# Sparse attention in a decoder step: page products divided among the single steps of the dense products

## The chip, the cores and the metric

The kernel runs on one core of a Trainium2 chip. The metric is the device time of one execution in microseconds. A core has five engines with instruction queues of their own: TensorE (PE in the profile; PEld is its weight load), VectorE (DVE), ScalarE (ACT), GpSimd (POOL) and SyncE (SP). Each queue is worked off in order; engines wait for each other through semaphores. TensorE's clock is granted at one of two levels, 2.4 GHz (1.00 in the profile) or 1.2 GHz (0.50).

## The reference

One inference step of a four-layer decoder for a prompt of 512 tokens and 8 sample sequences of one token, model width 1024. The layers' mixers are a gated recurrence, sparse attention, a state-space mixer and the recurrence again; each is followed by a squared-ReLU MLP. The change is in the sparse attention, layer 1:

```python
q, k, v, qi, ki, wi = split(x @ w_in)          # 8 heads of 128; indexer: 8 heads of 64
ki = layer_norm(ki)
score = sum_h wi[h] * relu(qi[h] . ki)         # indexer scores, per query and key
sel = top_k(score)                             # keys that this query may use
logits = q . K[sel] / sqrt(128) + rel_bias[bucket(distance)]
o = softmax(logits) . V[sel] @ w_out
```

For the prompt, K and V are those of the prompt itself. For a sample they are 256 cached positions, in two pages of 128 that a page table names, and its own. A sample's page products are matrix times vector: for each sample, head and page, a 128 x 128 block of the page times one query column (logits), and later a block of the value page times one column of probabilities (values).

## The kernel before

Activations stand with features on the partitions and the 520 tokens (512 and 8) in the free dimension. A dense product is cut into *tiles* of 128 output features. A tile takes one *chunk* of weights, 128 x 1024, and has eight *steps* `k` of 128 input features. To keep float32 accuracy in the faster float32r format, weights and activations are split into a high and a low part; a step is six TensorE instructions (two halves of 260 tokens, three products each, lines L1702 to L1704). `tile(n, T)` issues a whole tile, `part(n, T, ks)` only the steps `ks`.

Weight chunks come in order on SyncE's DMA queue into two `raw` slots (L416). For each chunk ScalarE makes the high part (`high_at`, L595), GpSimd the low part (`low_at`, L450); after that the raw slot is free and the load two chunks on may start. ScalarE also copies finished tiles out of PSUM (L865), so its queue, written out by hand, mixes splits of coming chunks, copies and the attention's own work, and each waits for the one ahead of it.

The sparse-attention layer is the function `dsa`. Counted by tiles:

- Tiles 0 to 4 are indexer keys and queries. After them TensorE makes the keys' mean and mean square (L1850, L1852) and waits for VectorE's variance (`ki_var`). It then issues the head weights of the indexer, 3 query blocks x 8 steps, with eight moving columns each (L1859), the same for the samples (L1863), and the products that spread the relative-position bias into rows (L1867, L1868). ScalarE waits for these, copies the head weights (L899, L901) and the bias rows (L904, L905) out and issues the DMA that writes the bias rows to DRAM (L907); only then does its loop over tiles 5 to 28 begin, with `high_at` of chunk 8. Tile 5 comes after all this on TensorE.
- Tiles 6 to 8 (attention queries) alternate, two steps at a time, with the prompt's index products (L1879), whose ReLUs ScalarE makes (L875) and VectorE weighs and sums; tiles 9 to 12 with the samples' (L1888, L1895).
- Tiles 13 to 20 are the attention keys. After each whole tile comes `page_logits(n)`, the 16 page products of sample `n` (L1906, two instructions each, 32 in the profile). VectorE works on the top-k meanwhile.
- Tiles 21 to 28 are the attention values, an iteration `it` each: two steps, then `slot(s)` with attention products of the prompt (logits L1929, turns L1941, values L1961). From `it` = 3 on, `page_values(it - 3)` (L1917, 32 instructions) stands ahead of the tile; the last three pages follow in the tail, after the last tile.

A sample's two pages fill one of two page slots. GpSimd issues their loads (`kv_pages`, L500) after it has split the chunk that is queued before them, and once `pages_used` tells that the sample two before has been used.

The lines that the change touches are in `dsa`:

Of the kernel before, what the change touches and what calls it, by code (L numbers as in the profile page):

```python
# [24 lines left out]
P = 128  # L25
D = 1024
KT = D // P
NP_ = 512
NS = 8
N = NP_ + NS  # L30
NH2 = N // 2
TB = NP_ // P
# [4 lines left out]
HEADS = 8  # L37
# [8 lines left out]
HN = HEADS * NS  # L46
# [59 lines left out]
def trunk(nc, I, O, kinds=KINDS):  # L106
# [3 lines left out]
    def sb(name, shape, dt=F32, c=ctx):  # L110
        return c.enter_context(nc.sbuf_tensor(name, shape, dt))

    def sem(name):
        return ctx.enter_context(nc.semaphore(name))
# [3 lines left out]
    c = ExitStack()  # L118
# [3 lines left out]
    c = ExitStack()  # L122
# [20 lines left out]
    c = ExitStack()  # L143
# [4 lines left out]
    c = ExitStack()  # L148
# [7 lines left out]
    c = ExitStack()  # L156
# [3 lines left out]
    c = ExitStack()  # L160
# [11 lines left out]
    c = ExitStack()  # L172
    mixB = sb("mixB", [P, KT, N], F32, c)
# [3 lines left out]
    pg = sb("pg", [P, 2, 2, D], F32, c)  # L177
# [4 lines left out]
    c = ExitStack()  # L182
# [91 lines left out]
    mb = ctx.enter_context(nc.psum_tensor("mb", [P, 4, 512], F32))  # L274
# [4 lines left out]
    tile_out = sem("tile_out")  # L279
# [31 lines left out]
    pg_loaded = [sem("b_pg_loaded0"), sem("b_pg_loaded1")]  # L311
# [75 lines left out]
    def low_count(n):  # L387

        before = sum(min(max(n - a, 0), b - a) for a, b in by_dve)
        if any(a <= n < b for a, b in by_dve):  # L390
            return w_low_dve, before + 1
        return w_low, n - before + 1
# [1293 lines left out]
    def _(pe):  # L1686
# [4 lines left out]
        def chunk(low, slot, T, hi, lo, k0, start, stop, split=None, ks=range(KT)):  # L1691

            if 0 in ks:
                pe.wait_ge(*low)
            for k in ks:
                if split is not None:
                    pe.wait_ge(xl_ready, split + k + 1)
                w = slice(k * P, (k + 1) * P)
                for half in range(2):
                    t = slice(half * NH2, (half + 1) * NH2)  # L1700
                    first, last = start and k == 0, stop and k == KT - 1
                    pe.matmul(bank(T, half), wh[:, slot, w], hi[:, k0 + k, t], start=first, stop=False)  # L1702
                    pe.matmul(bank(T, half), wh[:, slot, w], lo[:, k0 + k, t], start=False, stop=False)  # L1703
                    ins = pe.matmul(bank(T, half), wl[:, slot, w], hi[:, k0 + k, t], start=False, stop=last)  # L1704
            return ins

        def tile(n, T, split=None):

            if T >= 2:
                pe.wait_ge(tile_out, T - 1)  # L1710
            chunk(low_count(n), n % SPL, T, xh, xl, 0, True, True, split).then_inc(chunk_done, 1)

        def part(n, T, ks, split=None):

            if 0 in ks and T >= 2:
                pe.wait_ge(tile_out, T - 1)
            ins = chunk(low_count(n), n % SPL, T, xh, xl, 0, True, True, split, ks)
            if KT - 1 in ks:
                ins.then_inc(chunk_done, 1)
# [121 lines left out]
        def dsa(y, c0, t0):  # L1841
# [9 lines left out]
            for b in range(2):  # L1851
                ins = pe.matmul(mb[:, 2 + b, 0:NH2], ones_idx[:], rl[:, 0, b * NH2:(b + 1) * NH2], start=True, stop=True)  # L1852
            ins.then_inc(ki_stats, 1)

            pe.wait_ge(ki_var, 1)
            pe.wait_ge(x_ready, 16 * y["i"])
            for qb in range(1, TB):
                for k in range(KT):
                    pe.matmul(mb[:, 0, (qb - 1) * IH:qb * IH], x[:, k, qb * P:(qb + 1) * P], wwi[:, k, :],  # L1859
                              start=k == 0, stop=k == KT - 1)  # L1860
            for a in range(2):
                for k in range(KT):
                    ins = pe.matmul(mb[0:4, 1, a * NS:(a + 1) * NS], wwi[:, k, 4 * a:4 * a + 4], x[:, k, NP_:N],  # L1863
                                    start=k == 0, stop=k == KT - 1)
            ins.then_inc(wi_psum, 1)

            pe.matmul(mb[0:HEADS, 2, :], relb[:, 0:8], oh_p[:, 0:512], start=True, stop=True)  # L1867
            pe.matmul(mb[0:HEADS, 3, 0:ROW - 512], relb[:, 0:8], oh_p[:, 512:ROW], start=True, stop=True  # L1868
# [27 lines left out]
                                    stop=n == NS - 1 and a == 1)  # L1896
                ins.then_inc(s8_ready, 1)

            def page_logits(n):

                pe.wait_ge(pg_loaded[n % 2], 32 * (n // 2 + 1))
                pe.wait_ge(tile_out, t0 + 13)
                for g in range(2):
                    for h in range(HEADS):
                        col = g * HN + h * NS + n
                        ins = pe.matmul(mb[:, 3, col:col + 1], pg[:, n % 2, g, h * P:(h + 1) * P],  # L1906
                                        mixB[:, h, NP_ + n:NP_ + n + 1], start=True, stop=True)
                ins.then_inc(pages_used, 1)

            def page_values(n):  # L1910

                slot_ = (NS + n) % 2
                pe.wait_ge(pg_loaded[slot_], 32 * ((NS + n) // 2 + 1))
                for h in range(HEADS):
                    col = h * NS + n
                    for g in range(2):
                        ins = pe.matmul(pagev[:, col:col + 1], pg[:, slot_, g, h * P:(h + 1) * P],  # L1917
                                        sptt[:, g * HN + col:g * HN + col + 1], start=g == 0, stop=g == 1)
                ins.then_inc(pages_used, 1)

            def logits(u):
                h, qb = UNITS[u]
# [42 lines left out]
            def slot(s):  # L1965

                it, i = s // 4, s % 4
                if i == 1 and 1 <= it <= HEADS:
                    turn_values(it - 1, min(s - TURN, NU))
                if VALUE <= s:  # L1970
                    values(s - VALUE)
                if s < NU:
                    logits(s)
                if TURN <= s < NU + TURN:
                    turn(s - TURN)

            tile(c0 + 5, t0 + 5)
            pe.wait_ge(ki_ready, 1)
            pe.wait_ge(rows_out, 2)
            for c in range(6, 9):  # L1980
# [8 lines left out]
            for c in range(9, 13):  # L1989
                for i in range(4):  # L1990
                    n = 2 * (c - 9) + i // 2
                    part(c0 + c, t0 + c, (2 * i, 2 * i + 1))
                    (sample_dots, sample_sums)[i % 2](n)
            for c in range(13, 21):
                tile(c0 + c, t0 + c)
                page_logits(c - 13)
            for it in range(HEADS):
                c = 21 + it
                if it == 0:
                    pe.wait_ge(sneg_ready, 1)  # L2000
                    pe.wait_ge(s8_out, 1)
                    pe.matmul(mb[0:HN, 1, 0:SK], relb[:, 8:72], oh_p[:, ROW:ROW + SK], start=True, stop=False)
                    pe.matmul(mb[0:HN, 1, 0:SK], rep8, s8, start=False, stop=True).then_inc(sz_ready, 1)
                if it == 1:
                    pe.wait_ge(sz_out, 1)
                    pe.wait_ge(sprod, 1)
                    pe.matmul(mb[0:HN, 1, PAST:SK], sprodt, ones[:, 0:1], start=True, stop=True)
                    pe.wait_ge(slog, 1)
                    for g in range(2):
                        ins = pe.transpose(mb[0:HN, 1, g * P:(g + 1) * P], ltok[:, g * HN:(g + 1) * HN], ident[:])  # L2010
                    ins.then_inc(sy_ready, 1)
                if it == 2:
                    pe.wait_ge(sp_ready, 1)
                    for g in range(2):
                        pe.transpose(mb[:, 1, g * HN:(g + 1) * HN], sl[:, g * P:(g + 1) * P], ident[0:HN, 0:HN])
                    pe.matmul(mb[:, 1, P:P + HN], ones[0:HN, :], sdiag, start=True, stop=True).then_inc(spt_ready, 1)
                if it >= 3:
                    pe.wait_ge(spt_out, 1)
                    pe.wait_ge(sbc_out, 1)
                    page_values(it - 3)  # L2020
                for i in range(4):
                    part(c0 + c, t0 + c, (2 * i, 2 * i + 1))
                    slot(4 * it + i)
            for s in range(NU, NU + VALUE):
                slot(s)
                if s < NU + 3:
                    page_values(s - NU + 5)
# [3 lines left out]
        for y in plan:  # L2031
            ln = 2 * y["i"]
            c0, t0 = y["c"], y["t"]
# [21 lines left out]
            if y["kind"] == 1:  # L2055
                dsa(y, c0, t0)
                tail, ttail = c0 + 29, t0 + 29
# [77 lines left out]
            for half in range(2):  # L2135
# [17 lines left out]
                with pe.Fori(0, KT // 2) as i:  # L2153
                    for m in range(2):
                        T = t2 + m
                        pe.wait_ge(tile_out, i * 2 + T - 1)
                        for b in range(2):
                            n = c2 + 2 * m + b
                            low, count = low_count(n)
                            pe.wait_ge(h_ready, g1 + KT * (b + 1))  # L2160
                            ins = chunk((low, i * 4 + count), n % SPL, T, hh, hl, 8 * b, b == 0, b == 1)
# [131 lines left out]
```

## Time and profile before

| | |
|---|---|
| median of three runs | 3060.54 us (3057.29 to 3063.38) |
| profiled execution | 3046.29 us, span 3044.6 us |
| TensorE busy | 2844.6 us, 93% of the span |
| VectorE, ScalarE, GpSimd busy | 51%, 34%, 34% |
| mean granted clock of TensorE | 0.952 |
| DMA, mean | 97 GB/s |
| stage of tiles 13 to 20 | 940.79 to 1029.35 us of the span |
| iterations with a page, tiles 24 to 28 | 1065.63 to 1148.29 us of the span |

Times within the profile are microseconds from the start of the span. A busy TensorE is not one at full speed: the granted clock of a stretch has to be read beside it. Matmuls overlap, so the distance from one start to the next is what an instruction costs, not its length.

### The profile page before, as it was taken

To read this page: it belongs to the slowest core of one execution; us is meant where nothing else is said; L and a number is where in the kernel's file an instruction comes from. 1 tells how busy PE (TensorE), PEld (TensorE's weight loads), DVE (VectorE), ACT (ScalarE), POOL (GpSimd) and SP (SyncE) were. 2 spreads that over 40 slices of the span, in tenths; PEclk is the share of its full clock that TensorE was granted. 3 is DMA by queue.
4 is the path that set the end of the run, shared out by engine and by line. 5 is a ranking of instruction groups with operands and counts; after the bars stand their busy time and mean duration, and the time that the engine had idled before them with its cause. 6 is when DMAs were issued, how large, how long until landed. Compare 5 with 4: busy or idle time off the path is not lost. (4 is left out here: it accounts for less than half of the span.)

```text
span 3044.6 us, 54973 instructions
## 1 busy us (share of the span) xinstructions
PE 2844.6 (93%) x22296; PEld 2752.8 (90%) x22296; DVE 1550.8 (51%) x2208; ACT 1045.7 (34%) x1612; POOL 1037.7 (34%) x537
## 2 busy tenths in 40 slices
PE   7999799999889999999994798999999998899997
PEld 7999799999868999899994698999989997899997
DVE  4555356062235532789697936606245554471442
ACT  4555342122331343422214434212245455331222
POOL 2000164444523224544441145444530001554442
PEclk9999899999988898999996999999999998899999
DMA  4222123222253332224245522322232221232221
GB/s 147 82 82 72 37 84 97 90 90 96 91 103 117 141 124 72 93 95 145 90 158 187 170 74 76 97 92 94 91 95 79 78 85 51 64 97 91 92 94 63
DMA packets 125232, 294.81 MB, mean 97 GB/s; under 512 B 11058, under 2 KB 58674, under 8 KB 124946
## 3 DMA queue, kind: packets, MB, share of 16 engines
q1 hardware_dynamic: 56592, 206.10, 21.0%
q10 hardware_dynamic: 63362, 68.68, 7.5%
q0 software_dynamic: 5120, 17.83, 1.6%
q8 instruction: 110, 1.80, 0.2%
q14 instruction: 48, 0.39, 0.0%
HBM read 255.87 MB, written 36.70 MB: 96 GB/s over the span
## 5 line engine op out<-in xcount | busy, mean ns | idle before, releaser
L450 POOL TENSOR_TENSOR wl<-raw,wh 128x1024 fp32r<-128x1024 f32 x325 | 807.6, 2488 | 840.0 <-ACT wh L587 507.4
L1702 PE MATMUL lp<-xh,wh 128*128 128x260 f32 x3712 | 1077.8, 290 | 14.3 <-POOL wl L450 4.8
L1704 PE MATMUL lp<-xh,wl 128*128 128x260 f32 x3712 | 1061.0, 286 | 0.0
L1703 PE MATMUL lp<-xl,wh 128*128 128x260 f32 x3712 | 1058.4, 285 | 0.0
L1702 PEld LDWEIGHTS lp<-xh,wh 128*128 128x128 f32 x3712 | 712.6, 192 | 35.8 <-issue 22.4
L1703 PEld LDWEIGHTS lp<-xl,wh 128*128 128x128 f32 x3712 | 712.0, 192 | 0.4
L1704 PEld LDWEIGHTS lp<-xh,wl 128*128 128x128 f32 x3712 | 711.3, 192 | 0.0
L1702 PE MATMUL lp<-hh,wh 128*128 128x260 f32 x2048 | 578.6, 283 | 4.4 <-DVE r L1187 4.4
L1704 PE MATMUL lp<-hh,wl 128*128 128x260 f32 x2048 | 578.6, 283 | 0.0
L1703 PE MATMUL lp<-hl,wh 128*128 128x260 f32 x2048 | 576.8, 282 | 0.0
L1702 PEld LDWEIGHTS lp<-hh,wh 128*128 128x128 f32 x2048 | 385.4, 188 | 5.0 <-issue 5.0
L1704 PEld LDWEIGHTS lp<-hh,wl 128*128 128x128 f32 x2048 | 385.2, 188 | 0.0
L1703 PEld LDWEIGHTS lp<-hl,wh 128*128 128x128 f32 x2048 | 385.0, 188 | 0.0
L595 ACT ACTIVATE wh<-raw 128x1024 fp32r<-128x1024 f32 x213 | 223.9, 1054 | 261.8 <-PE lp L1704 123.5
L1674 DVE TENSOR_TENSOR hl<-lw,hh 128x520 f32 x128 | 292.4, 2284 | 15.8
L587 ACT ACTIVATE wh<-raw 128x1024 fp32r<-128x1024 f32 x176 | 185.8, 1056 | 268.7 <-PE lp L1704 208.9
L462 POOL TENSOR_TENSOR xl<-mixA,xh 128x520 fp32r<-128x520 f32 x16 | 20.8, 1332 | 671.0 <-ACT xh L601 671.0
L1130 ACT ACTIVATE lw<-lp 128x520 f32<-128x520 f32 x124 | 75.0, 605 | 447.9 <-PE lp L1704 425.1
L1189 DVE SCALAR_TENSOR_TENSOR r<-x,lp 128x520 f32<-128x520 f32 x56 | 39.0, 696 | 344.3 <-PE lp L1704 320.6
L1672 DVE TENSOR_TENSOR lw<-lw 128x520 f32<-128x520 f32 x128 | 115.4, 902 | 193.4 <-ACT lw L1130 189.3
L1729 PE MATMUL lp<-xh,wh 128*128 128x260 f32 x352 | 104.0, 320 | 75.4 <-ACT xh L601 31.7
L1729 PEld LDWEIGHTS lp<-xh,wh 128*128 128x128 f32 x352 | 77.2, 219 | 80.1 <-ACT xh L601 33.4
(352 smaller groups left out, 3546.5 us busy)
## 6 DMA issues: line engine op xcount, KB each, us to landing
raw<-in_wstream SPq DMA_DIRECT2D x389, 512.0 KB, 3.5
s<-in_s_in ACTq DMA_DIRECT2D x16, 512.0 KB, 5.7
out_hg_s<-s ACTq DMA_DIRECT2D x16, 512.0 KB, 3.3
pg<-in_kpages POOLq DMA_DIRECT2D x16, 512.0 KB, 5.3
pg<-in_vpages POOLq DMA_DIRECT2D x16, 512.0 KB, 5.4
s_q<-pqb ACTq DMA_DIRECT2D x8, 640.0 KB, 3.9
qn<-s_q ACTq DMA_DIRECT2D x8, 640.0 KB, 5.4
s_rot<-lw ACTq DMA_DIRECT2D x8, 512.0 KB, 2.6
```

What stands on the lines that cost most here:

```text
L450: pool.tensor_tensor(wl[:, s, :], raw[:, r_, :], wh[:, s, :].bitcast(F32), ALU.subtract).then_inc(w_low, 1)
L462: pool.tensor_tensor(xl[:, m, :], src[:, m, :], xh[:, m, :].bitcast(F32), ALU.subtract).then_inc(xl_ready, 1)
L587: act.activation(wh[:, s, :], raw[:, r_, :], ACT.Copy).then_inc(w_high, 1)
L595: act.activation(wh[:, n % SPL, :], raw[:, n % RAW, :], ACT.Copy).then_inc(w_high, 1)
L1130: act.activation(halves(lw[:, 6 + c % 2, :]), out_banks(T, half == 0 and i is first and c == 2), ACT.Relu).then_inc(tile_out, 1)
L1189: dve.scalar_tensor_tensor(halves(r[:, m, :]), halves(x[:, m, :]), ALPHA, src, ALU.mult, ALU.add).then_inc(tile_out, 1)
L1672: link.step(dve.tensor_tensor(hq, lw[:, 6 + c % 2, :], lw[:, 6 + c % 2, :], ALU.mult))
L1674: dve.tensor_tensor(lo, hq, hi.bitcast(F32), ALU.subtract).then_inc(h_ready, 1)
L1702: pe.matmul(bank(T, half), wh[:, slot, w], hi[:, k0 + k, t], start=first, stop=False)
L1703: pe.matmul(bank(T, half), wh[:, slot, w], lo[:, k0 + k, t], start=False, stop=False)
L1704: ins = pe.matmul(bank(T, half), wl[:, slot, w], hi[:, k0 + k, t], start=False, stop=last)
L1729: pe.matmul(out, wh[:, slot, w], xh[:, k, t], start=k == 0, stop=False)
```

## The change

Three edits on TensorE's queue; the instructions are the same ones in another order, and no other engine's program changes.

1. Page logits: after each single step of tiles 13 to 20 come the products of one head (two page products, four instructions), in place of all 16 products after the tile. The wait for the sample's pages stands ahead of head 0, so after the tile's first step.
2. Page values: in the iterations 3 to 7, one head's products after each step, in place of all of them ahead of the tile. The three pages of the tail stay as they were.
3. Index head weights: steps 0 and 1 of tile 5 are put ahead of the wait for `ki_var`; the other six steps stand singly between groups of head-weight products, four steps of a query block each, and around the two halves of the samples' products. The bias-row products come after all of tile 5.

```diff
+            part(c0 + 5, t0 + 5, (0, 1))
             pe.wait_ge(ki_var, 1)
             pe.wait_ge(x_ready, 16 * y["i"])
-            for qb in range(1, TB):
-                for k in range(KT):
+
+            def head_weights(qb, ks):
+
+                for k in ks:
                     pe.matmul(mb[:, 0, (qb - 1) * IH:qb * IH], x[:, k, qb * P:(qb + 1) * P], wwi[:, k, :],
                               start=k == 0, stop=k == KT - 1)
-            for a in range(2):
+
+            def sample_head_weights(a):
+
                 for k in range(KT):
                     ins = pe.matmul(mb[0:4, 1, a * NS:(a + 1) * NS], wwi[:, k, 4 * a:4 * a + 4], x[:, k, NP_:N],
                                     start=k == 0, stop=k == KT - 1)
-            ins.then_inc(wi_psum, 1)
+                if a == 1:
+                    ins.then_inc(wi_psum, 1)
+
+            for qb in range(1, TB):
+                head_weights(qb, range(4))
+                part(c0 + 5, t0 + 5, (2 * qb,))
+                head_weights(qb, range(4, KT))
+                if qb == 3:
+                    sample_head_weights(0)
+                part(c0 + 5, t0 + 5, (2 * qb + 1,))
+            sample_head_weights(1)
...
-            def page_logits(n):
-
-                pe.wait_ge(pg_loaded[n % 2], 32 * (n // 2 + 1))
-                pe.wait_ge(tile_out, t0 + 13)
+            def page_logits(n, h):
+
+                if h == 0:
+                    pe.wait_ge(pg_loaded[n % 2], 32 * (n // 2 + 1))
+                    pe.wait_ge(tile_out, t0 + 13)
                 for g in range(2):
-                    for h in range(HEADS):
-                        col = g * HN + h * NS + n
-                        ins = pe.matmul(mb[:, 3, col:col + 1], pg[:, n % 2, g, h * P:(h + 1) * P],
-                                        mixB[:, h, NP_ + n:NP_ + n + 1], start=True, stop=True)
-                ins.then_inc(pages_used, 1)
-
-            def page_values(n):
+                    col = g * HN + h * NS + n
+                    ins = pe.matmul(mb[:, 3, col:col + 1], pg[:, n % 2, g, h * P:(h + 1) * P],
+                                    mixB[:, h, NP_ + n:NP_ + n + 1], start=True, stop=True)
+                if h == HEADS - 1:
+                    ins.then_inc(pages_used, 1)
+
+            def page_values(n, hs=range(HEADS)):
 
                 slot_ = (NS + n) % 2
-                pe.wait_ge(pg_loaded[slot_], 32 * ((NS + n) // 2 + 1))
-                for h in range(HEADS):
+                if 0 in hs:
+                    pe.wait_ge(pg_loaded[slot_], 32 * ((NS + n) // 2 + 1))
+                for h in hs:
...
-            tile(c0 + 5, t0 + 5)
             pe.wait_ge(ki_ready, 1)
             pe.wait_ge(rows_out, 2)
...
             for c in range(13, 21):
-                tile(c0 + c, t0 + c)
-                page_logits(c - 13)
+                for k in range(KT):
+                    part(c0 + c, t0 + c, (k,))
+                    page_logits(c - 13, k)
...
                 if it >= 3:
                     pe.wait_ge(spt_out, 1)
                     pe.wait_ge(sbc_out, 1)
-                    page_values(it - 3)
                 for i in range(4):
-                    part(c0 + c, t0 + c, (2 * i, 2 * i + 1))
+                    for k in (2 * i, 2 * i + 1):
+                        part(c0 + c, t0 + c, (k,))
+                        if it >= 3:
+                            page_values(it - 3, (k,))
                     slot(4 * it + i)
```

## Rows read from the trace of the kernel before

**Rows 1.** The page, sections 1 and 2: TensorE's share, its granted clock by slice.

```profile
PE 2844.6 (93%) x22296; PEld 2752.8 (90%) x22296; DVE 1550.8 (51%) x2208; ACT 1045.7 (34%) x1612; POOL 1037.7 (34%) x537
...
PEclk9999899999988898999996999999999998899999
```

**Rows 2.** Windows of tiles 13 to 20: length, TensorE busy, granted clock, DMA.

```profile
950.15:961.00 10.85, 10.85 (x83) 0.84 0.42 145
...
983.12:995.16 12.04, 12.04 (x82) 0.75 0.39 131
...
sum 88.56, PE 88.56; mean PE 11.07
```

**Rows 3.** Timeline of TensorE, end of tile 13: start, length, operation.

```profile
946.54 0.28 PE L1704 MATMUL lp<-xh,wl 128*128 128x260 f32 x1
946.66 3.63 PE L1906 MATMUL mb<-mixB,pg 128*128 128x1 f32 x32
950.15 0.37 PE L1702 MATMUL lp<-xh,wh 128*128 128x260 f32 x1
950.35 0.28 PE L1703 MATMUL lp<-xl,wh 128*128 128x260 f32 x1
950.47 0.28 PE L1704 MATMUL lp<-xh,wl 128*128 128x260 f32 x1
...
951.92 0.42 PE L1703 MATMUL lp<-xl,wh 128*128 128x260 f32 x1
```

**Rows 4.** Windows of the five iterations with a page of values.

```profile
1065.63:1080.90 15.27, 15.27 (x124) 1.00 0.40 139
...
sum 82.66, PE 82.66; mean PE 16.53
```

**Rows 5.** Timeline of TensorE, head weights, bias rows, start of tile 5.

```profile
842.84 7.75 PE L1859 MATMUL mb<-bsm,x 128*128 128x8 f32 x48 [2.26 <-DVE lw L1504]
...
851.40 1.87 PE L1867 MATMUL mb<-oh_p,relb 32*8 32x512 f32 x2
...
853.63 0.59 PE L1702 MATMUL lp<-xh,wh 128*128 128x260 f32 x1
```

**Rows 6.** Windows: head weights, samples' index stage, two steps behind the eighth page.

```profile
842.84:845.79 2.95, 2.95 (x27) 1.00 0.63 243
845.79:853.63 7.84, 7.84 (x60) 0.50 0.35 118
...
910.65:940.79 30.14, 30.14 (x202) 1.00 0.18 57
...
1030.55:1033.32 2.77, 2.77 (x14) 0.50 0.98 339
```

**Rows 7.** Timeline of ScalarE: bias write issued, chunk 8 split, chunk 10 split.

```profile
854.51 0.81 ACTq L907 DMA_DIRECT2D bias_rows<-bsm  x1
855.73 1.06 ACT L595 ACTIVATE wh<-raw 128x1024 fp32r<-128x1024 f32 x1 [1.25 <-issue]
...
879.54 1.06 ACT L595 ACTIVATE wh<-raw 128x1024 fp32r<-128x1024 f32 x1 [7.25 <-DMA raw<-in_wstream]
```

**Rows 8.** Weight loads: all of the page, then the one issued at 859.4.

```profile
raw<-in_wstream SPq DMA_DIRECT2D x389, 512.0 KB, 3.5
...
raw<-in_wstream SPq DMA_DIRECT2D x1, 512.0 KB, 20.1
```

**Rows 9.** Timeline of TensorE: around the first index products, and the wait.

```profile
863.39 0.28 PE L1704 MATMUL lp<-xh,wl 128*128 128x260 f32 x1
863.61 0.70 PE L1879 MATMUL mb<-lw,qi 64*128 64x256 f32 x4
...
881.03 1.64 PE L1879 MATMUL mb<-lw,qi 64*128 64x384 f32 x3 [3.34 <-ACT lw L875]
```

**Rows 10.** Second page load issued for tile 16; landing of that pair.

```profile
963.49 0.53 POOL L500 DMA_DIRECT2D pg<-in_kpages  x1 [0.58 <-issue]
...
DMA to landing us min/median/max: 5.2/5.6/5.9
```

More of the change, by code:

```diff
@@ L1918, in page_values @@
                                         sptt[:, g * HN + col:g * HN + col + 1], start=g == 0, stop=g == 1)
-                ins.then_inc(pages_used, 1)
+                if HEADS - 1 in hs:
+                    ins.then_inc(pages_used, 1)
             def logits(u):
```

## The prediction

> **What bounds the kernel now.** The page comes first: TensorE is busy 93% of the span, so time is won only where TensorE waits or runs slow, and the clock line shows dips among the nines [rows 1]. Cut by tile, the stage of the eight key tiles, each followed by its page's products, shows where: no idle time in 88.56 us, but the granted clock averages 0.75 to 0.84 in seven of the eight stretches [rows 2]. The timeline tells why: 32 page products, one moving column each, take 3.49 us at 1.00; dense work resumes at 950.15, and by 951.92 its instructions last 0.42 in place of 0.28: the clock has fallen to 0.50 behind the block [rows 3]. The value tiles repeat it: of five iterations with a page the first took 15.27 us at 1.00, the other four 67.39 together, 16.85 each [rows 4].
>
> The head-weight stretch is another matter. TensorE waits 2.26 us for VectorE, then issues 48 head-weight products, 32 for the samples and the bias-row products, before tile 5 [rows 5]; the clock is 0.50 after the first 2.95 us [rows 6]. But TensorE does not set the pace there. ScalarE copies the bias rows out once the last bias product is done, issues their write to DRAM at 854.51, and only then, its queue being in order, splits chunk 8 at 855.73 [rows 7]. That split frees the raw slot for chunk 10, whose load is issued at 859.4 and lands 20.1 us later, against a median of 3.5 [rows 8]. ScalarE stands 7.25 us at 879.54 for it [rows 7], and TensorE waits 3.34 us until 881.03 for the ReLUs queued behind that split [rows 9]. So from 854 to 881 the chain is: last bias product, bias write, split 8, load 10, split 10, ReLUs. Tile 5 lies beside it, not on it.
>
> **The change, part by part.**
>
> *Page logits.* No product is added or removed; each dense step (6 instructions) is now followed by 4 page instructions. Dense instructions start 0.12 apart, the first after page products takes 0.20, the first page product follows a dense one after 0.12, and a page instruction takes 3.49/32 = 0.109 [rows 3]. A step is 0.20 + 5 x 0.12 + 4 x 0.109 = 1.24 us, a tile 9.89, eight 79.1. Of 88.56 that saves 9.5 us, if the clock stays at 1.00. This is itself a balance: full speed for seven tiles gives back some 14, and 56 more returns from page to dense at 0.08 cost 4.5.
>
> The clock of that mix is not in the trace. Its nearest row is the sample stage, where runs of 12 dense instructions alternate with sample products that use a few rows or columns of the array: 1.00 throughout 30.14 us [rows 6]. The other end is the page block itself. I take 1.00, since two thirds of a new step (0.80 of 1.24 us) is dense, as there, and no narrow run is longer than 0.44 us against 3.49.
>
> *The pages' landing.* A page's slot is free at the same point as before, the end of the tile two before, but the page is now needed after the first step of its tile, not after the last. The page used in tile 16 is loaded after the split queued before it on GpSimd: its second half is issued at 963.49 and takes up to 5.9 us, to 969.4 [rows 10]. The tile that set this off ended 3.49 before 961.00 [rows 2], at 957.5: 11.9 us. The other five pages come to 10.6 to 11.8. The new order needs it 0.44 + 9.89 + 0.80 = 11.1 us after that point. The largest deficit is 0.8 us, and a wait in one tile is slack in the next, so I charge 1.5 us in all; bounds 0 and 4 (each of six waiting its worst). Left: 8.0.
>
> *The tile behind.* The first twelve dense instructions after the eighth page took 2.77 us at 0.50 [rows 6]; at 1.00 they take 0.20 + 11 x 0.12 = 1.52. With no block ahead of them: 1.2 us.
>
> *Page values.* Each of five iterations gets four more page-to-dense returns: 15.27 + 4 x 0.08 = 15.6, five are 78.0, against 82.66 [rows 4]: 4.7 us. Between the parts lie the attention products, full 128-wide work, so I hold 1.00 here too; the lower bound is a loss of 0.3 an iteration with no dip removed. Pages are freed an iteration later than before, but the next use is then 15.6 us away and landing needs some 8 (two issues, then 5.9 [rows 10]): hidden. The three pages of the tail stay blocks, and I price the tail at nothing; its clock may fall differently by 1.5 us either way.
>
> *Head weights.* Twelve dense instructions (1.5 us) fill the wait for VectorE: free, being hidden by that 2.26 us [rows 5]. From 842.84 to the end of the bias products it was 10.8 us. Now, at full clock: 48 x 0.109 (27 in 2.95 us [rows 6]) = 5.2; 36 dense in six groups, 6 x 0.80 = 4.8; sample products 0.9, from the end of the 48 to the bias products; these 1.1, half of their 2.23 [rows 5]; 12.0 us. The bias write starts 1.2 us later. Tile 6 could start some 6 us sooner, but its ReLUs still stand behind load 10, so the chain to 881 moves by +1.2: a loss. What is late next is everything after it by the same amount, for load 12 is issued after split 10 in turn. If the clock falls there as it did, 2.95 us in, the rest runs at half: 32 head-weight products at twice 0.109, 27 dense at 0.23 (2.77/12 [rows 6]), 0.9 and 2.23 make 16.3; the write moves by 2.95 + 16.3 - 10.8 = +8.5. I take +1.2: half of the new stretch is dense and the idle gap ahead is mostly filled; both ends stay in the range.
>
> **The sum.** 8.0 + 1.2 + 4.7 - 1.2 = 12.7 us. The profiled execution (3046.29, span 3044.6) would become 3033.6. The median of the runs is 3060.54, 14.25 above it; I carry that difference over: **3047.8 us**.
>
> On the load's 20.1 us [rows 8] the Trainium skill has a rule, in "DMA: Bandwidth & Descriptors", section "Queues, rings and completion order": each DMA engine goes round its queues, one packet of descriptors at a time. By that rule a weight load would share with the bias write from its start and chunk 10 would come within a few microseconds; the measured 20.1 us is against it. What it would give is rival B.
>
> **The rivals.**
>
> *A: the clock falls in the head-weight stretch.* Place, chain and price as above: 13.9 - 8.5 = 5.4 us saved, 3055.1. For it: the stretch starts behind an idle gap, and narrow products did drop the clock there [rows 6]. Against: six dense groups that were not there.
>
> *B: load 10 does not follow the bias write,* but shares with it. Then TensorE keeps what tile 5 gives it: tile 6 started 12 x 0.12 before 863.61 [rows 9], at about 862.1, and could start at 842.84 + 12.0 + 1.4 for ScalarE's copies = 856.3. That is +5.8 in place of -1.2: 3040.8. Against it stands the 20.1 us.
>
> *C: every change of kind is dear on both sides.* Before the index products, which use 64 rows, the last dense instruction holds TensorE 0.22 in place of 0.12 [rows 9]. If the short page runs meet that too, 56 + 20 + 6 new entries at 0.1 cost 8.2: 4.5 left, 3056. Against: the entry into the page block is 0.12 [rows 3].
>
> *D: slower.* The thinned steps no longer keep the clock up, and the whole key stage runs at 0.50: a step is then 6 x 0.23 + 4 x 0.218 = 2.25 us, 1.0 more than at 1.00; 64 of them add 65 to the 79.1, so the stage loses 56 where 9.5 were won. With the rest of the sum, about 3113. It decides from 13 steps of the 64 at half clock, which eat the 12.7. For it: page products alone did this. Against: the sample stage.
>
> **How the numbers follow.** A measurement of this kernel tells about 0.2% (6.1 us) from no change. Chances: the forecast 0.50, A 0.28, C 0.08, B 0.06, D 0.05, none of these 0.03. Faster by over 0.2%: nearly all of the forecast, all of B, under half of A, a third of C: 0.69. Within: the rest of A and C and a little of the forecast: 0.20. Slower: D, and the unlucky ends of A and C with page waits at their bound: 0.11. The range runs from B's 3041 to A with 4 us of page waits, 3059; the forecast's own range is 3044 to 3052.
>
> **What would show it.** Right: the eight key tiles take 79 to 83 us at 1.00; value iterations 15.6; page-to-dense starts 0.20 and dense-to-page 0.12; ScalarE's wait for the chunk-10 load ends as much later as the last bias product does, and TensorE's wait ahead of the index products is longer than 3.34. Wrong: 0.50 inside the key tiles; page waits over 1 us in each tile; or the ReLUs after chunk 10 coming earlier than before, measured from the normalisation ahead. Most of all the forecast depends on the clock in the 12 us of the head-weight stretch.

## The result, and the profile after

The changed kernel takes 3035.24 us (median of 12 runs, 3022.81 to 3055.43) against 3060.28 us of the kernel before (12 runs, 3053.55 to 3068.90): a ratio of 0.9927, interval 0.9905 to 0.9948, so 22.3 us faster, 16 to 29 (the two medians themselves lie 25.0 apart). The forecast had the sign and the mechanism, but 12.7 us in place of 22, and the measured time lies below its range of 3041 to 3059. The profiled execution took 3034.24 us, span 3032.6.

From the page of the changed kernel, TensorE's share and its granted clock by slice; the 13th and 14th digit, where tiles 9 to 23 lie, are now nines, and were eights in [rows 1]:

```profile
PE 2828.2 (93%) x22296; PEld 2733.6 (90%) x22296; DVE 1551.0 (51%) x2208; ACT 1045.2 (34%) x1612; POOL 1039.0 (34%) x537
...
PEclk9989989999989998999996999999999998899999
```

Windows of the changed kernel, tiles 13 to 20 (length, busy time of PE, PEld, DVE, ACT, POOL, granted clock, DMA share, GB/s). All eight stand at 1.00 and sum to 76.17 us, where [rows 2] had 88.56, seven of the eight at 0.75 to 0.84:

```profile
950.71:960.05 9.34, 9.34 (x82) 9.34 (x81) 7.71 (x27) 1.06 (x3) 2.37 (x1) 1.00 0.38 114
...
979.01:988.71 9.70, 9.61 (x83) 9.40 (x82) 9.18 (x24) 1.57 (x3) 3.42 (x3) 1.00 0.46 162
...
sum 76.17, PE 75.96 PEld 74.98 DVE 66.01 ACT 12.04 POOL 26.31; mean PE 9.50 PEld 9.37 DVE 8.25 ACT 1.51 POOL 3.29
```

The same for the five iterations with a page of values, 76.07 us against 82.66 in [rows 4]:

```profile
1062.20:1077.39 15.19, 15.19 (x126) 14.25 (x124) 6.48 (x24) 6.99 (x17) 2.64 (x2) 1.00 0.21 70
...
sum 76.07, PE 76.07 PEld 71.37 DVE 32.44 ACT 34.96 POOL 16.96; mean PE 15.21 PEld 14.27 DVE 6.49 ACT 6.99 POOL 3.39
```

The timeline of one step of the changed kernel answers to [rows 3]. The first dense instruction behind a page run holds TensorE 0.20 (960.05 to 960.25), as forecast. But the page run of four lasts from 960.86 to 961.22, 0.36 us, not 4 x 0.109 = 0.44:

```profile
960.05 0.37 PE L1702 MATMUL lp<-xh,wh 128*128 128x260 f32 x1
960.25 0.29 PE L1703 MATMUL lp<-xl,wh 128*128 128x260 f32 x1
...
960.73 0.28 PE L1704 MATMUL lp<-xh,wl 128*128 128x260 f32 x1
960.86 0.50 PE L1921 MATMUL mb<-mixB,pg 128*128 128x1 f32 x4
961.22 0.37 PE L1702 MATMUL lp<-xh,wh 128*128 128x260 f32 x1
```

In the head-weight stretch the clock held this time. The windows of the changed kernel go from the first head weight to the bias rows, and, behind the bias rows, over the first steps of tile 6 and the first index products, where it stood at 0.50:

```profile
852.75:863.68 10.93, 10.93 (x116) 10.70 (x117) 2.58 (x3) 2.17 (x3) 4.86 (x6) 1.00 0.37 132
...
866.11:871.00 4.89, 4.89 (x20) 4.01 (x21) 0.35 (x1) 3.15 (x5) 2.62 (x2) 0.50 0.36 41
```

The chain of [rows 7 to 9] is there again. ScalarE of the changed kernel issues the bias write, then splits chunk 8, and later waits 12.31 us for chunk 10:

```profile
866.01 0.81 ACTq L907 DMA_DIRECT2D bias_rows<-bsm  x1
867.24 1.06 ACT L595 ACTIVATE wh<-raw 128x1024 fp32r<-128x1024 f32 x1 [1.25 <-issue]
...
891.03 1.06 ACT L595 ACTIVATE wh<-raw 128x1024 fp32r<-128x1024 f32 x1 [12.31 <-DMA raw<-in_wstream]
```

and TensorE waits for the ReLUs behind that split, 8.40 us where [rows 9] had 3.34:

```profile
892.51 2.03 PE L1894 MATMUL mb<-lw,qi 64*128 64x384 f32 x4 [8.40 <-ACT lw L875]
```

To set the parts side by side, TensorE's starts in every profile of this study were cut at the same six points: the keys' mean (L1850), the first key tile, the opening of the value stage (tile 21), the first value tile with a page (24), the instruction behind the last dense one of tile 28, and the first dense product behind the tail. The table holds the times between them, in us; how each kernel differs stands with its experiment.

| kernel | mean to key tiles | key tiles | tiles 21 to 23 | tiles 24 to 28 | tail | sum |
|---|---|---|---|---|---|---|
| before | 102.20 | 88.56 | 36.28 | 81.13 | 28.64 | 336.8 |
| after | 102.21 | 76.17 | 35.33 | 74.10 | 28.27 | 316.1 |
| e1_keys | 104.43 | 76.08 | 35.42 | 81.15 | 28.76 | 325.8 |
| e2_values | 104.68 | 88.50 | 36.18 | 74.10 | 29.21 | 332.7 |
| e3_heads | 103.25 | 88.56 | 37.84 | 82.68 | 29.44 | 341.8 |
| e4_pages | 104.65 | 76.93 | 35.35 | 74.10 | 31.93 | 323.0 |
| g2 | 102.33 | 77.56 | 35.56 | 74.10 | 29.14 | 318.7 |
| g16 | 112.20 | 74.65 | 36.20 | 74.10 | 32.22 | 329.4 |
| c1 | 95.30 | 75.90 | 35.35 | 74.10 | 28.28 | 308.9 |
| c2 | 100.55 | 76.11 | 35.31 | 74.10 | 31.57 | 317.7 |
| h1 | 103.86 | 75.94 | 35.35 | 74.10 | 31.55 | 320.8 |
| t1 | 102.04 | 76.38 | 35.34 | 84.82 | 12.31 | 310.9 |
| best | 103.86 | 76.42 | 35.33 | 84.82 | 13.51 | 313.9 |
| best2 | 99.64 | 75.90 | 35.34 | 84.82 | 13.51 | 309.2 |

The two profiled executions differ by 20.7 us between these points (336.8 and 316.1), but by only 12.05 in all: ahead of the keys' mean, where the program is the same, the changed kernel's took 9.9 us more (848.50 against 838.59). That this profile, 3034.24 us, lies next to the 3033.6 that the prediction worked out for it is therefore luck.

### The profile page after: what moved, and what is told of

The parts are those of the page before. It is cut to its first block and busy times, and to the rows that moved or that the text cites. A ratio compares the mean times of both kernels' runs of the same rounds, so it can differ in the third digit from the quotient of the medians.

```text
span 3032.6 us, 54973 instructions
## 1 busy us (share of the span) xinstructions
PE 2828.2 (93%) x22296; PEld 2733.6 (90%) x22296; DVE 1551.0 (51%) x2208; ACT 1045.2 (34%) x1612; POOL 1039.0 (34%) x537
## 5 line engine op out<-in xcount | busy, mean ns | idle before, releaser
L1703 PEld LDWEIGHTS lp<-xl,wh 128*128 128x128 f32 x3712 | 704.5, 190 | 0.5
L1704 PEld LDWEIGHTS lp<-xh,wl 128*128 128x128 f32 x3712 | 703.6, 190 | 0.0
```

## The experiments

**The three edits one by one.** Each kernel is the one before with only the parts named; undone parts keep the old place of the products.

```diff
# e1_keys: edit 1 alone
-                tile(c0 + c, t0 + c)
-                page_logits(c - 13)
+                for k in range(KT):
+                    part(c0 + c, t0 + c, (k,))
+                    page_logits(c - 13, k)
# e2_values: edit 2 alone
-                    page_values(it - 3)
...
+                        if it >= 3:
+                            page_values(it - 3, (k,))
# e3_heads: edit 3 alone (head weights and tile 5); e4_pages: edits 1 and 2
```

> Only the page logits divided among the steps of tiles 13 to 20; head weights and page values as before. Theory T (what the two profiles show): a run of four page instructions takes 0.36 us inside dense work, not 0.44, so the eight key tiles fall from 88.6 to 76 us at a granted clock of 1.00, and with the tile behind them this part is worth 13 to 14 us: ratio 0.9955 to 0.9960. Rival P (the prices of the prediction, and something else made the rest of the gain): 9.2 us, key tiles 79 to 83 us, ratio 0.9970. Rival H (the gain comes from the head weights' new place): ratio above 0.998.

> Only the page values of tiles 24 to 28 divided among the steps; the rest as before. Theory T: the five iterations fall from 82.7 to 76 us at 1.00, and the tail keeps a little: 6.5 to 7.5 us, ratio 0.9975 to 0.998. Rival P: 4.7 us, ratio 0.9985. Rival H: no change, 0.9995 to 1.0005.

> Only the head weights divided (steps 0 and 1 of tile 5 ahead of the wait for the variance, the other six between the groups); the pages as before. Theory T: TensorE's wait ahead of the index products grows from 3.3 to some 8 us and eats what the filled gap and the full clock give; 0 to 2 us slower, ratio 0.9995 to 1.0007. Rival P: 1.2 us slower. Rival H (the moved bias write meets the weight loads at a better moment, or the clock stays up in the index stage): 5 us or more faster, ratio below 0.9985.

> Page logits and page values divided, head weights as before: the change without its third edit. Theory T: the sum of the two parts, 20 to 21 us, ratio 0.9930 to 0.9935, the same as the whole change's 0.9927 within the measurement. Rival P: 13.9 us, ratio 0.9955. Rival H: less than half of the whole change's 22 us, ratio above 0.9965.

Measured against the kernel before: e1_keys 0.9951 (0.9923 to 0.9980), e2_values 0.9997 (0.9975 to 1.0020), e3_heads 1.0004 (0.9981 to 1.0028), e4_pages 0.9947 (0.9921 to 0.9972). The head weights alone bring nothing that can be measured, and the page logits carry most of the gain. H meets none of these ratios, though the ends of two intervals (0.9981 of e3_heads, 0.9972 of e4_pages) touch its limits. T and P differ by some 4 us for the logits and less for the values, which these intervals of 15 us can't tell apart. The ratio of e2_values shows no gain, and its lower end, 7.7 us, just reaches T; its median, 3051.89 us, stands 10.5 below the 3062.34 of the kernel before beside it, so its runs leave the values open. The windows do tell the theories apart. Key tiles of e1_keys:

```profile
942.92:1019.00 76.08, 75.59 (x642) 74.89 (x641) 65.99 (x176) 12.05 (x17) 26.42 (x22) 1.00 0.45 159
```

tiles 24 to 28 of e2_values:

```profile
1067.14:1141.25 74.11, 74.11 (x602) 69.94 (x601) 32.36 (x120) 34.62 (x84) 16.70 (x13) 1.00 0.41 126
```

Wherever the logits are divided step by step the key tiles take 75.9 to 76.9 us, and 88.5 to 88.6 wherever they are not divided; with one page to an iteration tiles 24 to 28 take 74.10 with the values divided, against 81.1 to 82.7. P's 79 to 83 us for the key tiles is met by none. Of the values' gain the tail gives some back: 28.6 to 29.4 us (before, e1_keys, e3_heads) with the old order, 28.3 to 32.2 with the new one, in which the last page run of tile 28, some 0.4 us, lies behind the cut.

Why the times scatter by 15 us and more while these windows repeat to the hundredth can be read further on in the profiles. One head of the second gated recurrence, untouched by any edit, in the kernel before:

```profile
2332.15:2358.27 26.12, 25.71 (x203) 23.75 (x202) 11.51 (x19) 10.25 (x17) 0.00 (x0) 1.00 0.28 84
```

the same head in e4_pages:

```profile
2312.08:2339.77 27.69, 27.28 (x203) 25.32 (x202) 11.49 (x19) 10.23 (x16) 0.00 (x0) 0.94 0.26 79
```

and in e3_heads:

```profile
2338.61:2371.05 32.44, 32.02 (x203) 29.59 (x202) 11.49 (x19) 10.23 (x16) 0.00 (x0) 0.79 0.21 68
```

The same instructions take 26.1, 27.7 or 32.4 us, by whether and when the clock falls in them, and there are eight such heads. So an execution's time says little about a few microseconds elsewhere.

**What a change of kind costs.** Both kernels are the whole change with the page logits cut finer or coarser. They and c1, c2, h1 and t1 below ran once each, so only their windows are read, not their times.

```diff
# g2: one page product after each half step (inside the dense loop)
+                    if after is not None:
...
+                        after(k, half)
# g16: the products of four heads after every four steps
-                for k in range(KT):
-                    part(c0 + c, t0 + c, (k,))
-                    page_logits(c - 13, k)
+                for i in range(2):
+                    part(c0 + c, t0 + c, range(4 * i, 4 * i + 4))
+                    for h in range(4 * i, 4 * i + 4):
+                        page_logits(c - 13, h)
```

> The whole change, with the page logits divided twice as finely: one page product (two instructions) after every half step of three dense instructions, 128 short runs in place of 64. In the changed kernel the eight key tiles take 76.2 us, 1.16 a step. Theory L: TensorE goes at one pace per instruction there, some 0.116 us each whatever its kind, and a change of kind costs nothing; the 0.20 after a page run is made good by a page run that is 0.08 short. Then the tiles take 76 us again, up to 77. Rival P (the price of the prediction): every return from page to dense work costs 0.08; 64 more make 81.3 us. The granted clock is 1.00 for both.

> The whole change, with the page logits divided in two halves only: the products of four heads (16 instructions) after every four steps of a key tile, 16 runs in place of 64. Theory L: no price for a change of kind; 74.5 to 76.2 us for the eight key tiles, the lower end because a page is needed after step 3 and its waits vanish; provided that the granted clock stays at 1.00 with narrow runs of 1.8 us. Rival P: 48 returns fewer at 0.08 and no page waits, 71 to 72 us. Rival K: a narrow run of this length already drops the clock as the one of 32 did, and the tiles take 80 to 88 us at 0.75 to 0.9.

Timeline of g2, and the window of its key tiles:

```profile
960.51 0.28 PE L1925 MATMUL mb<-mixB,pg 128*128 128x1 f32 x2
960.65 0.37 PE L1702 MATMUL lp<-xh,wh 128*128 128x260 f32 x1
...
962.52 0.38 PE L1925 MATMUL mb<-mixB,pg 128*128 128x1 f32 x2 [0.68 <-DMA pg<-in_kpages]
```

```profile
942.50:1020.06 77.56, 75.72 (x641) 75.09 (x640) 67.45 (x176) 11.84 (x17) 26.33 (x22) 1.00 0.44 155
```

and of g16:

```profile
950.71 1.84 PE L1921 MATMUL mb<-mixB,pg 128*128 128x1 f32 x16
952.41 0.36 PE L1702 MATMUL lp<-xh,wh 128*128 128x260 f32 x1
```

```profile
947.74:1022.39 74.65, 74.65 (x642) 74.64 (x641) 66.19 (x177) 12.89 (x18) 26.41 (x22) 1.00 0.47 166
```

A page run of 2, 4, 16 or 32 instructions lasts 0.14, 0.36, 1.70 or 3.49 us, from its first start to the next dense one. Each time that is n x 0.112 less 0.08: 0.14, 0.37, 1.71, 3.50. The 0.08 that the first dense instruction takes longer is what the page run ahead of it is short: a shift at the seam, not a price. The 640 instructions of g16's key tiles take 74.65 us, 0.117 each on the mean. g2, with 128 seams in place of 64, spends 1.4 us more than the changed kernel, not P's 5.1. Most of that is page waits: it needs the page half a step sooner, and three waits of 0.96, 1.03 and 0.69 us start to start stand in its timeline (the first is the one of 0.68 idle above). They are 2.6 us beyond its other runs; in the changed kernel six page runs are late, by 0.16 to 0.36 us, 1.55 in all. The 0.3 that is left makes under 0.01 us for each of the 64 seams. P also missed g16, by 3 us. Theory L held, and K fell: with narrow runs of 1.7 us the clock stayed at 1.00 in this profile. g16's gain of 1.5 over the changed kernel is the page waits: none of its runs is late, the page being needed after step 3 and not after step 0.

PEld's row of the changed kernel shows the one pace: a weight load 0.11 to 0.12 after the other, the four of a page run 0.45 in all, and the first of them starting with the last dense product still moving (the ends of products are modelled in the profile):

```profile
960.62 0.19 PEld L1704 LDWEIGHTS lp<-xh,wl 128*128 128x128 f32 x1
960.74 0.53 PEld L1921 LDWEIGHTS mb<-mixB,pg 128*128 128x128 f32 x4
961.19 0.19 PEld L1702 LDWEIGHTS lp<-xh,wh 128*128 128x128 f32 x1
```

The Trainium skill, "TensorE: Matmul & The Clock Gate", section "LDWEIGHTS (loading the stationary operand)", puts a load at its columns divided by 1.2 in nanoseconds, 107 for 128; the 112 of a page instruction agrees with that within 5%. That the loads set the pace is read from this agreement and the even spacing; no run here took a load away.

**The chain behind the bias write.** Both kernels are the whole change with ScalarE's order altered.

```diff
# c1: split chunk 8 before the wait for the head weights
+                high_at(c0 + 5 + AHEAD)
                 act.wait_ge(wi_psum, 1)
# c2: as c1, and ahead of the bias rows' copies
+                copy_tile(5, mixB[:, 0, :])
+                high_at(c0 + 6 + AHEAD)
                 act.wait_ge(rows_ready, 1)
```

> The whole change, and ScalarE splits chunk 8 before it waits for the head weights, so before the bias rows are copied and written to DRAM. Theory W (the chain of the prediction): TensorE's wait of 8.7 us ahead of the index products stands at the end of bias write, split 8, load 10. Now load 10 is issued some 9 us sooner, ahead of the write, and lands in 4 to 6 us in place of 20.1; the wait ahead of the index products falls below 2 us, loads 11 and 12 still take 15 to 21 us and give back at most 3 us. From the keys' mean to the first key tile the time falls from 102 us to 94 to 97. Rival V: VectorE's or ScalarE's work on the index scores sets the pace there, and the wait only turns into others: 100 us or more.

> As the run before, and ScalarE also copies tile 5 out and splits chunk 9 before it copies the bias rows and issues their write. Theory W: the write starts some 1.5 us later, load 11 is issued some 5 us sooner, with the write, and lands in less than its 21.4 us; another 0 to 3 us less than the run before between the keys' mean and the first key tile. Rival V: the same time as the run before, or more by the 1.5 us by which the write is later.

c1's ScalarE splits chunk 8 at 852.39, and the bias write follows at 860.98:

```profile
852.39 1.06 ACT L595 ACTIVATE wh<-raw 128x1024 fp32r<-128x1024 f32 x1 [0.72 <-ACT lw L894]
...
860.98 0.81 ACTq L908 DMA_DIRECT2D bias_rows<-bsm  x1
```

Chunk 10's load is issued at 856.08, ahead of the write, and lands in 3.5 us; chunk 11's, issued at 865.99 behind it, takes 19.9 (DMA issues of c1 in those two stretches):

```profile
raw<-in_wstream SPq DMA_DIRECT2D x1, 512.0 KB, 3.5
...
raw<-in_wstream SPq DMA_DIRECT2D x1, 512.0 KB, 19.9
```

Around the prompt's index products no wait over 1.76 us is left on TensorE, the one ahead of tile 9, and the time from the mean to the key tiles falls from 102.2 to 95.30 us, inside W's 94 to 97. So the chain is as the prediction had it: what delays the load is being issued behind the write, and what TensorE waits for is that load. V fell, though a part of it is there: ahead of the samples' sums TensorE now waits 3.02 us for ScalarE, where the changed kernel waited 1.74.

```profile
911.12 1.88 PE L1912 MATMUL mb<-bsm 4*8 4x257 f32 x4 [3.02 <-ACT bsm L926]
```

The trace also shows how a load behind the write comes to take 19.9 us: half of it is quick. From 866.5 to 869.7 us SyncE's queue (q1) moves 0.26 MB, half of chunk 11; from 869.7 to 877.5 the write's queue (q10) moves alone, with 47.5% of the engines' time; the other half comes among the write's packets, from 877.5 on. The queues of c1 in the first two of these windows:

```profile
q1 hardware_dynamic: 72, 0.26, 28.2%
...
q10 hardware_dynamic: 152, 0.39, 47.5%
```

That fits a write that holds half of the DMA engines, but the profile does not name the engines. The Trainium skill, "DMA: Bandwidth & Descriptors", section "Queues, rings and completion order", has each DMA engine drain a whole packet of one queue before it turns to the next. That rule alone does not promise that a load behind a write lands within a few microseconds, as the prediction took it; half of this load did and half did not, and how the write is cut into packets no run here shows.

c2 leaves no wait over 1.17 us there, and 2.83 ahead of the samples' sums. But its load 11, now issued at 861.43 and 1.3 us behind the write, took 20.1 us, and its clock fell in the head-weight stretch, which hides what its second step is worth: 100.55 us from mean to key tiles.

**The head-weight stretch and the tail.** h1 adds thinner head weights to c2; t1 adds the tail's pages to the whole change; best has both; best2 has no third edit.

```diff
# h1: three (or two) products of the head weights, then one step of tile 5 or 6
+            for qb in range(1, TB):
+                for ks in ((0, 1, 2), (3, 4, 5), (6, 7)):
+                    head_weights(qb, ks)
+                    step()
# t1: pages 1 to 6 two to an iteration, none in the tail
+                        if it in (3, 7):
+                            page_values(7 * (it // 7), (k,))
+                        elif it > 3:
+                            page_values(2 * it - 7 + k // 4, (2 * (k % 4), 2 * (k % 4) + 1))
...
-                if s < NU + 3:
-                    page_values(s - NU + 5)
# GpSimd issues the pages' loads to match
+                    for u in {24: (10,), 25: (11, 12), 26: (13, 14), 27: (15,)}.get(c, ()):
+                        kv_pages(u)
# best: h1 and t1; best2: e4_pages, c1 and t1
```

> The whole change with ScalarE's order of run c2, and the head weights thinned further: three of their products (six instructions), then one dense step, nine times, the dense steps being tile 5's other six and the first steps of tile 6; the fourth step of tile 6 follows the bias-row products, and tile 6's last four steps then take two index products each. From the keys' mean to the first key tile c1 took 95.0 us with the clock at 1.00 in the head-weight stretch, c2 100.2 us with the clock fallen to 0.50 early in it. Theory S (the share of narrow work decides whether the clock holds there): it holds, 92 to 95 us. Rival F (the clock falls there in some executions, whatever stands between the groups): 98 to 101 us if it is met in this one.

> The whole change, and the three pages of the tail are taken into the iterations: one page in the iterations 3 and 7, two in 4 to 6 (two heads after each step), their loads issued accordingly; the tail has no page products. From the first value tile with a page to the first dense product behind the tail the changed kernel took 102.4 us, 26.3 of them in the tail, most of it at 0.50. Theory B (the blocks of 32 take the clock down there, as they did in the key tiles): three pages cost 3.7 us each in the iterations, the tail keeps 8 to 12.4 us; 95 to 99.5 us in all. Rival Q: the blocks cover waits of the tail's own chain, turn, copy and value products, which now show: 101 us or more. Rival R: the second page of an iteration comes late, and TensorE waits over 1 us for it three times.

> Both runs before together: thinned head weights, chunks 8 and 9 split ahead of the bias write, no pages in the tail. If theories W, S and B hold, the changed kernel loses some 8 us between the keys' mean and the key tiles and 3 to 7 us in the values: 3020 to 3026 us, ratio 0.987 to 0.990 against the kernel before. If the clock falls in the head-weight stretch all the same, 5 us more in those executions; if rival Q holds, nothing from the tail: 3028 us, 0.991.

> Page logits and page values divided, no page left in the tail, chunk 8 split ahead of the bias write; the head weights as in the kernel before, without the third edit. What the runs so far show: the clock of the divided head-weight stretch held in five of nine profiles and fell in four, and where it fell the time from the keys' mean to the first key tile grew by 5 to 10 us; thinning it further did not keep it. Theory N (the third edit brings 2 us at best and costs up to 10): from the keys' mean to the first key tile 96 to 98 us, against 103.5 in the run best, and the whole as fast as best or up to 5 us faster, ratio 0.9855 to 0.9875. Rival M (the third edit is worth its place on the mean of the executions): 3 us or more slower than best, ratio above 0.988.

The stretch from the first head weight to the bias rows, the same code in g16 and c1, and thinned in h1. In g16:

```profile
839.78:856.77 16.99, 16.99 (x117) 16.66 (x117) 2.83 (x3) 2.17 (x3) 4.99 (x6) 0.58 0.27 96
```

in c1:

```profile
847.46:858.40 10.94, 10.94 (x117) 10.71 (x117) 2.59 (x3) 3.23 (x4) 7.24 (x7) 1.00 0.47 161
```

and in h1:

```profile
839.06:860.08 21.02, 21.02 (x134) 20.75 (x134) 2.60 (x3) 4.78 (x6) 9.60 (x8) 0.56 0.36 121
```

In five of the nine profiles with the third edit (the changed kernel, e3_heads, g2, c1, t1) this stretch took 10.9 to 11.2 us at 0.95 to 1.00; in four (g16, c2, h1, best) the clock fell in it. It cost 6.1 us in the stretch itself (16.99 against 10.93) and 10 us by the key tiles (112.20 against 102.21), where chunk 10 waits for the later write. h1 and best have more dense steps there and fell both: theory S is out, and F stands as far as two profiles go, though both took 103.86 us from mean to key tiles, over its 98 to 101. In the five kernels that keep the old order the clock fell there every time (0.52 to 0.67 over the head weights). What decides it stays open; busy time and clock in the 40 us ahead look alike in both kinds.

The tail of the changed kernel, and t1's windows over tiles 24 to 28 and its tail:

```profile
1136.30:1164.58 28.28, 25.43 (x156) 24.20 (x154) 3.19 (x11) 5.66 (x14) 2.16 (x4) 0.70 0.26 84
...
1047.69:1132.51 84.82, 84.82 (x698) 80.65 (x696) 38.96 (x120) 35.32 (x84) 18.51 (x17) 1.00 0.42 135
1132.51:1144.82 12.31, 7.85 (x60) 6.48 (x58) 3.18 (x11) 5.56 (x14) 0.00 (x0) 1.00 0.06 22
```

97.13 us in place of 102.37: three pages cost 10.7 in the tiles, 3.6 each, and the tail is 16.0 shorter and now at 1.00, where it stood at 0.70. Theory B held. Some of Q is there, TensorE idle for 4.5 of the tail's 12.31 us, but it does not outweigh it; R did not show.

best ran in 3018.95 us (four runs), ratio 0.9871, interval 0.9843 to 0.9899, the fastest of this study and clear of the changed kernel's interval. Its forecast of 3020 to 3026 us rested on theory S, which failed, so that the ratio came out as forecast is in part luck. best2 came to 3022.91 us (six runs), 0.9902, 0.9875 to 0.9928. From mean to key tiles best2 took 99.64 us, more than N's 96 to 98, and its ratio lies on M's side; but the intervals of best and best2 overlap, and best's profile had the fallen clock. Whether the third edit is worth its place is not settled.

## Why the prediction was right or wrong

**Right: the mechanism and the clock.** The gain is the granted clock's: 1.00 in all key tiles and all value iterations. Rival D, the thinned steps losing the clock, did not come, and the sample stage [rows 6] was the right row to judge the mix by. The size was not right: of the signs that it named, the starts of 0.20 and 0.12 and the longer wait ahead of the index products came, but the key tiles took 76.17 us in place of 79 to 83, and the value iterations 15.21 in place of 15.6.

**The step that failed: the price of a return to dense work.** "56 more returns from page to dense at 0.08 cost 4.5", and 4 x 0.08 in each value iteration. The 0.20 in [rows 3] is real, but the block of 32 there was already 0.08 short, and 3.49/32 = 0.109 hid it. Taking the long interval at one side of a seam as a cost, and the average of the block as its pace, charged the seam twice. Without it the eight key tiles come to 79.1 - 4.5 = 74.6 us, and g16, which has no page waits, took 74.65; five iterations come to 78.0 - 1.6 = 76.4, measured 76.07. That is 6.1 of the 9.6 us between the 12.7 forecast and the 22.3 measured. Rival C, every change of kind dear on both sides, was the same error taken further: a page run still follows a dense instruction after 0.12.

**Right: the page waits.** 1.5 us were charged; the late page runs come to 1.55, and 76.17 less g16's 74.65 is 1.5.

**The tile behind, and the tail.** Charged 1.2; tiles 21 to 23 fall from 36.2 to 37.8 us to 35.3 to 35.6 (36.2 in g16), so 1 to 2.5. The tail was priced at nothing, 1.5 either way; it gives back some 1.3 on the mean (28.9 over before, e1_keys and e3_heads; 30.3 over the eight others that keep its pages), 0.4 of it the page run behind the cut. Values and tail together bring 81.6 - 74.1 - 1.3 = 6.2 us on the mean, for 4.7.

**Head weights: the chain right, the term too low.** The prediction had the point at which the ReLUs let TensorE go on 1.2 us later; from the keys' mean it went from 42.44 to 44.01 us, 1.6 later. By the key tiles this is gone: 102.0 to 103.3 us with the edit while the clock holds, 102.2 to 104.7 without. So the 1.2 us charged as a loss is a gain of 1.5 on the mean while the clock holds; with g16, where it fell, the mean of five profiles (the changed kernel, e3_heads, g2, g16, t1) is 0.4 worse than without the edit. Rival B is refuted: the wait grew, and c1 shows the write's place in it, though half of a load does share with the write. Rival A is real, but it is not another outcome of the kernel: it is met in some executions and not in others, four profiles of nine, so it belongs in the spread. Of the changed kernel's 12 times, seven lie between 3022.8 and 3036.2 us and five between 3046.5 and 3055.4. A gap of 10 us fits a clock that falls in that stretch in some of them; since single runs have no trace, this is not shown.

**The sum, and what was carried over.** By the means of the table the parts are 12.3 (key tiles), some 1.4 (behind) and 6.2 (values and tail), 19.9 us, with 1.5 for the head weights while the clock holds and -0.4 with g16 in the mean: 19.5 to 21.4 us, beside 22.3 by the ratio and its interval of 16 to 29. The difference of 14.25 us from the profiled execution to the median is the same as taking the 12.7 from the median, so it adds nothing to the miss; but it shows how little one profile says of a time. For the changed kernel the difference is 1.0. The profiled execution of before was a lucky one, 7 us below the fastest of its 12 timed runs (four of the 35 beside the first experiments were faster still), and its windows sum to 336.8 us where the undivided stages of all profiles average 339.9.

## What to carry to other kernels

Narrow products that stand in a long block are worth spreading among dense ones for the clock alone, down to a step or up to half a tile apart, and the seams cost next to nothing (under 0.01 us each in g2); spread them so that their data is needed late (half a tile apart took 1.5 us less than step by step). To price a short run of one kind inside another, take starts over whole periods, both seams included. And a load that must not be late is issued before a large write to DRAM, not behind it: one split moved ahead in ScalarE's queue was worth 6.9 us from the mean to the key tiles (c1 against the changed kernel), and some 4 with the old order of the head weights (best2 against the mean of before, e1_keys, e2_values and e4_pages); each is one profile.

## What the runs showed of the hardware that was not expected

- Dense float32r instructions with 260 moving columns and page instructions with one take nearly the same time in a mixed stream, 0.120 and 0.112 us: 640 in 74.65 us, 0.117 each.
- The same code at the same place holds the granted clock in one execution and loses it in another (10.9 and 17.0 us for one stretch; 26.1, 27.7 and 32.4 for one head of the recurrence), and nine dense steps in place of six between the head weights did not hold it.
- A 512 KB load issued 1.3 to 5 us behind the bias write took 19.9 to 20.1 us, one issued 4.9 us ahead of it 3.5. In c1 half of the late load's bytes moved in the first 3.7 us behind its issue.
